# A two-block transformer kernel: attention rounds joined into one row of steps, and score matmuls on 64 partition rows

## The chip, the cores and the metric

One core of one Trainium2 chip runs the whole program. TensorE is called PE, VectorE DVE, ScalarE ACT, GpSimd POOL, SyncE SP. The metric is device time in microseconds (us) of one execution, median of several runs.

## The reference

Two transformer blocks on 512 tokens of 1024 channels, everything in float32. Of the first block only the three attentions matter here, of the second the sparse attention and a small cross attention:

```
A (diff_attention): 4 heads, each two maps of 64 channels; chunked causal mask
    p = softmax(q k^T * scale);  a = p[map 0] - lam * p[map 1];  o = a @ v (128 channels), then rmsnorm
B (chunk_band_attention): 8 heads of 64; a bias table for each head is added to the scores
C (memory_attention): 4 heads of 128, 256 memory rows
N (nsa_mixer): 16 heads of 64 in 4 groups that share keys and values; for each head
    o = g_c * softmax_c(q kc) vc + g_s * softmax_s(q ks) vs + g_w * softmax_w(q kw) vw
    c: 31 compressed keys; s: selected blocks (all, at this length); w: window (causal)
X (cross_attention): 4 heads of 64, 256 memory rows
```

Around them stand the projections, a gated recurrent branch and the feed-forward layers, which make up most of the time.

## The kernel before

The program is written engine by engine, in one order fixed by hand for each engine; semaphores join them. Projections are float32 split into a high and a low part, with three matmuls for one (`mm3`, L914 to L916): ACT rounds the raw weight tile (`act_split`, L621), DVE makes the rest (`dve_split`, L628), SP loads the next.

The attentions run in the order A, B, C, later N0, N1, X. Each is a loop over rounds (`its`: A 2, B 4, C 2, N0 2, N1 2, X 2), and a round has 16, 8, 8, 36, 36 and 8 steps. A step is one tile of 128 queries against all its keys for one head (and map or branch); `step_of` says which, `width` how many keys. A step goes through five stations:

1. PE: the score matmul into PSUM bank 4 + t % 4 (L733; L730 for the four small ones of a c step), once the bank's last step was read (`s_masked`).
2. DVE: adds the mask or bias, takes the row maximum and writes the scores to `Sm` (L865; c steps L854 to L857).
3. ACT: exp with the row sum (L790; c steps L784).
4. DVE: reciprocal (L890) and multiplication with it (L900 for B, C and X, L897 with a gate for N, L894 for A's second map, which also adds the first).
5. PE transposes it `lag` slots after the scores (L748; c steps L745; lag 4 for A, N, X, 3 for B, C), ACT copies the result to SBUF (`PT`, `PTr` or `PTnr`: L813, L810, L806).

When both steps of a map (in A and C all of a head's) are through, PE multiplies with the values two slots later (L1076 in A, L1084 for pairs of 64-wide heads in B, N and X, which write to two halves of the partitions, L1093 in C, L1104 in c steps); two slots after that ACT copies the output of a finished group (L836; in A L832, behind the squares of L829).

The slots run from 0 to the round's steps plus lag, so every round ends with its last transposes and products before the next begins. Ahead of a round DVE stages: `stage_a` to `stage_x` copy the queries (L1928, L1954, L1964, L2176, L2187) into four tiles `QZ` or `QZn`, of which the other 64 partition rows were set to zero by POOL (L503, L562), so that a matmul over 128 rows sees only one head's 64 channels; B and C also copy values into `vst` (L1955, L1965). PE waits for `staged` before its first slot. The bias tiles of B are made by POOL (L515) in two buffers, from two raw tiles that it loads itself. B's four rounds are a hardware loop; the other rounds are written out.

Of the kernel before, what the change touches and what calls it, by code (L numbers as in the profile page):

```python
# [107 lines left out]
def build(nc, a, out):  # L108

    ctx = ExitStack()  # L110
    with ctx:
# [59 lines left out]
        vst = place("vst", [P, TT, P], at=S_at + 10240)  # L171
# [31 lines left out]
        QZ = [place(f"QZ{s}", [P, T]) for s in range(4)]  # L203
        bias2 = [bias, place("bias1", [P, T])]
# [45 lines left out]
        top[0] = arena + 16384  # L250
        QZ2 = [place(f"QZn{s}", [P, T]) for s in range(4)]
# [172 lines left out]

        for n, its, steps, turns, maps, groups in (("A", 2, 16, 8, 2, 2), ("B", 4, 8, 8, 4, 1), ("C", 2, 8, 8, 2, 2),
                                                   ("N0", 2, 36, 36, 18, 2), ("N1", 2, 36, 36, 18, 2),
                                                   ("X", 2, 8, 8, 4, 1)):
            staged0 = attn_at[last]["stage0"] + attn_at[last]["its"] if attn_at else 0
            attn_at[n] = dict(its=its, n=steps, S0=atc[0], T0=atc[1], M0=atc[2], O0=atc[3], turns=turns, maps=maps, groups=groups, stage0=staged0)
            last = n  # L430
            atc = [atc[0] + its * steps, atc[1] + its * turns, atc[2] + its * maps, atc[3] + its * groups]
        s_full, s_taken, s_masked, s_exp, s_norm = (sem(x) for x in ("s_full", "s_taken", "s_masked", "s_exp", "s_norm"))
        t_full, t_free, pv_done, o_free, staged = (sem(x) for x in ("t_full", "t_free", "pv_done", "o_free", "staged"))
        bias_ready, pair_ready = sem("bias_ready"), sem("pair_ready")
        oa_sq, oa_sd, oa_ready = (sem(x) for x in ("oa_sq", "oa_sd", "oa_ready"))
        for n, per in (("A", 24), ("B", 8), ("C", 8), ("N0", 76), ("N1", 76), ("X", 8)):
            attn_at[n]["order"] = per
# [51 lines left out]
        def _(pool):  # L489
# [9 lines left out]
            for z in range(4):  # L499
                half = slice(64, 128) if z % 2 == 0 else slice(0, 64)  # L500

                pool.wait_ge(sq_used, 2 + 16) if z == 0 else pool.wait_ge(qz_zero, z)
                pool.memset(QZ[z][half, :], 0.0).then_inc(qz_zero, 1)  # L503

            for h in range(8 + 2):
                if h >= 2:
                    b = bias2[h % 2]
                    if h < 4:

                        pool.wait_ge(o_free, O_RING + attn_at["B"]["O0"])  # L510
                    else:

                        pool.wait_ge(s_masked, attn_at["B"]["S0"] + 8 * ((h - 2) // 2))
# [45 lines left out]
            for z in range(4):  # L559
                half = slice(64, 128) if z < 2 else slice(0, 64)  # L560
                pool.wait_ge(qz_zero, 4 + z)
                pool.memset(QZ2[z][half, :], 0.0).then_inc(qz_zero, 1)  # L562
            for h in range(2):
                pool.wait_ge(qz_zero, 8 + h)
                pool.memset(PTc[h][:, :], 0.0).then_inc(qz_zero, 1)
# [83 lines left out]
        def lag_of(kind):  # L649

            return 4 if kind in "ANX" else 3

        def S_of(kind, t):

            return Sm[t % (lag_of(kind) + 1)]

# [21 lines left out]
        def pt_of(kind, m):  # L678

            if not paired(kind):  # L680
                return PT[m % 2]
            if kind == "N" and m % 9 == 0:
                return PTc
            ring = PTr if kind == "B" else PTr2
            return [ring[:, m % 4, h, :] for h in range(2)]

        def group_of(kind, m):

            return m if kind in ("A", "C") else m // 9 if kind == "N" else 0

        def pt_free(A, kind, i, m):

            if not paired(kind):
                return M_(A, i, m) + (PV_RING - 1)
            if m < 4:

                return M_(A, i, 0) + PV_RING
            return M_(A, i, m) + (PV_RING - 3)

        def S_(A, i, t):  # L700
            return i * A["n"] + (A["S0"] + t)

        def T_(A, i, u):
            return i * A["turns"] + (A["T0"] + u)

        def M_(A, i, m):
            return i * A["maps"] + (A["M0"] + m)

        def O_(A, i, g):
            return i * A["groups"] + (A["O0"] + g)  # L710

        def pe_attention(pe, name, q_of, k_of, v_of):
            kind = name[0]
            A = attn_at[name]
            lag = lag_of(kind)
            stage0 = A["stage0"]

            def body(i):

                pe.wait_ge(staged, i + (stage0 + 1))  # L720
                for slot in range(A["n"] + lag):
                    if slot < A["n"]:
                        t = slot
                        h, m, qt = step_of(kind, t)
                        bank = ps[4 + t % 4]

                        pe.wait_ge(s_masked, S_(A, i, t) + (1 - S_RING)) if not (isinstance(i, int) and S_(A, i, t) < S_RING) else None
                        if m == "c":
                            for q in range(TT):
                                mm = pe.matmul(bank[:, q * NC32:(q + 1) * NC32], q_of(i, h, m, q), k_of(i, h, m, NC32), start=True, stop=True)  # L730
                        else:
                            n = width(kind, m, qt)
                            mm = pe.matmul(bank[:, 0:n], q_of(i, h, m, qt), k_of(i, h, m, n), start=True, stop=True)  # L733
                        mm.then_inc(s_full, 1)
                    t = slot - lag
                    if t >= 0 and turned(kind, t):
                        h, m, qt = step_of(kind, t)
                        u = turn_no(kind, t)
                        bank = ps[u % 2]

                        pe.wait_ge(s_norm, S_(A, i, t) + 1)
                        pe.wait_ge(t_free, T_(A, i, u) + 1)
                        if m == "c":
                            for q in range(TT):
                                mm = pe.transpose(bank[0:NC32, q * P:(q + 1) * P], S_of(kind, t)[:, q * NC32:(q + 1) * NC32], ident)  # L745
                        else:
                            for kc in range(width(kind, m, qt) // P):
                                mm = pe.transpose(bank[:, kc * P:(kc + 1) * P], S_of(kind, t)[:, kc * P:(kc + 1) * P], ident)  # L748
                        mm.then_inc(t_full, 1)

                    for te in ((t - 2, t - 1, t) if t == A["n"] - 1 else (t - 2,)):
                        m = last_of_map(kind, te) if te >= 0 else None
                        if m is None:
                            continue
                        g = group_of(kind, m)
                        u = turn_no(kind, te)

                        pe.wait_ge(t_free, T_(A, i, u) + (T_RING + 1))
                        if A["groups"] == 1:
                            if m == 0:  # L760
                                pe.wait_ge(o_free, O_(A, i, g) + O_RING)
                        elif kind != "N" or m % 9 == 0:
                            pe.wait_ge(o_free, O_(A, i, g) + 1)
                        obank = ps[2 + g % 2]
                        src = pt_of(kind, m)
                        mm = v_of(i, m, src, obank)
                        mm.then_inc(pv_done, 1)
            loop(pe, A["its"], body)

        def act_attention(act, name, o_to):  # L770
            kind = name[0]
            A = attn_at[name]
            lag = lag_of(kind)

            def body(i):
                for slot in range(A["n"] + lag - 1):
                    if slot < A["n"]:
                        t = slot
                        h, m, qt = step_of(kind, t)
                        n = width(kind, m, qt)  # L780

                        act.wait_ge(s_masked, S_(A, i, t) + 1)
                        if m == "c":
                            act.activation(S_of(kind, t)[:, 0:n], S_of(kind, t)[:, 0:n], ACT.Exp).then_inc(s_exp, 1)  # L784
                        else:
                            if m == "w":

                                at = (52 if qt == TT - 1 else 8) + t % 4
                                act.activation(st[:, 48 + t % 4:49 + t % 4], st[:, at:at + 1], ACT.Exp)
                            act.activation(S_of(kind, t)[:, 0:n], S_of(kind, t)[:, 0:n], ACT.Exp, bias=st[:, 8 + t % 4:9 + t % 4],  # L790
                                           scale=-1.0, accum_out=st[:, 12 + t % 4:13 + t % 4]).then_inc(s_exp, 1)
# [1512 lines left out]
```

## Time and profile before

| | us |
|---|---|
| median of 3 runs (2486.73 to 2488.80) | 2488.52 |
| the profiled execution | 2489.62 |
| its span, first to last instruction | 2487.8 |
| PE busy | 2324.6 (93%) |
| DVE busy | 1236.3 (50%) |
| ACT busy | 981.3 (39%) |
| POOL busy | 148.0 (6%) |
| matmuls of L914 to L916 in the chain that ended last | 70% |

The granted TensorE clock is 0.975 of full in the mean; a stretch shows it in tenths or as a share, where 0.5 is the lower of its two levels, 1.2 GHz of 2.4. Busy time counts a matmul from its start until its end has been modelled, so overlapping matmuls join into one piece; start times tell more than durations. Idle time is printed behind a row with what ended it.

### The profile page before, as it was taken

What the parts mean: (1) busy time and instruction counts of PE and PEld (TensorE: products, weight loads), DVE (VectorE), ACT (ScalarE), POOL (GpSimd) and SP (SyncE); (2) the same over time, 40 slices, a digit from 0 to 9 for tenths busy, and PEclk for the clock granted to TensorE, in tenths of its full rate; (3) what the DMA queues carried; (4) which work ended last, traced back from release to release, by engine and by line L of the source; (5) the groups of instructions that cost most, each with busy time, mean ns of one, the idle gap of its engine ahead of it and who ended that gap; (6) DMA issues with size and microseconds to landing.
All of it is one profiled execution on the core that took longest, in us unless ns stands there. A gap on an engine that the chain in (4) does not pass through costs nothing.

```text
span 2487.8 us, 30044 instructions
## 1 busy us (share of the span) xinstructions
PE 2324.6 (93%) x10984; PEld 1852.2 (74%) x10984; DVE 1236.3 (50%) x2264; ACT 981.3 (39%) x1621; POOL 148.0 (6%) x126
## 2 busy tenths in 40 slices
PE   5899999978887999999999989988999999999997
PEld 4788888766655777888888777766666688888886
DVE  4433335664455455444434647653888655432432
ACT  5432223454555333433223422623677633421321
POOL 1000002100010000100001420000000001000011
PEclk9999999989998999999999999999999999999998
DMA  5332333311200322332332372222000133233231
GB/s 186 105 101 76 110 95 88 112 52 43 68 9 26 101 93 93 102 101 79 107 100 79 90 233 80 68 71 76 14 1 1 42 95 101 86 102 101 85 101 51
DMA packets 213465, 206.72 MB, mean 83 GB/s; under 512 B 4832, under 2 KB 194400, under 8 KB 213120
## 3 DMA queue, kind: packets, MB, share of 16 engines
q1 hardware_dynamic: 210368, 192.31, 24.7%
q0 software_dynamic: 3008, 13.24, 1.6%
q8 instruction: 54, 0.88, 0.1%
q14 instruction: 35, 0.29, 0.0%
HBM read 199.25 MB, written 4.19 MB: 82 GB/s over the span
## 4 chain that ended last, share of the span: by engine, by line
PE 84%; DVE 8%; ACT 4%; issue 2%; DMA 2%; POOL 0%; SPq 0%; DVEq 0%; ACTq 0%; POOLq 0%
PE ps L914 24%; PE ps L916 23%; PE ps L915 23%; PE ps L733 4%; PE ps L1084 2%; PE ps L748 2%; DVE wlo L628 2%; ACT whi L621 2%; DMA wraw<-in_w_in 1%; DVE Sm L865 1%; PE ps L1119 1%; PE ps L730 1%; PE ps L1076 1%; DMA xin<-in_x 1%; PE ps L1144 0%
## 5 line engine op out<-in xcount | busy, mean ns | idle before, releaser
L628 DVE TENSOR_TENSOR wlo<-wraw,whi 128x2048 fp32r<-128x2048 f32 x192 | 440.4, 2294 | 425.1 <-ACT whi L621 425.1
L914 PE MATMUL ps<-hH,whi 128*128 128x512 f32 x1528 | 600.9, 393 | 19.0 <-DVE wlo L628 14.9
L916 PE MATMUL ps<-hH,wlo 128*128 128x512 f32 x1528 | 596.6, 390 | 0.0
L915 PE MATMUL ps<-hL,whi 128*128 128x512 f32 x1528 | 596.6, 390 | 0.0
L621 ACT ACTIVATE whi<-wraw 128x2048 fp32r<-128x2048 f32 x192 | 366.9, 1911 | 471.9 <-PE ps L916 441.3
L914 PEld LDWEIGHTS ps<-hH,whi 128*128 128x128 f32 x1528 | 287.6, 188 | 89.1 <-DVE wlo L628 21.6
L915 PEld LDWEIGHTS ps<-hL,whi 128*128 128x128 f32 x1528 | 287.7, 188 | 60.8 <-issue 1.0
L916 PEld LDWEIGHTS ps<-hH,wlo 128*128 128x128 f32 x1528 | 287.5, 188 | 61.0
L914 PE MATMUL ps<-gH,whi 128*128 128x512 f32 x608 | 236.5, 389 | 0.0
L915 PE MATMUL ps<-gL,whi 128*128 128x512 f32 x608 | 236.5, 389 | 0.0
L916 PE MATMUL ps<-gH,wlo 128*128 128x512 f32 x608 | 236.5, 389 | 0.0
L914 PE MATMUL ps<-whi,hH 128*128 128x512 f32 x352 | 140.9, 400 | 19.8 <-DVE wlo L628 9.4
L790 ACT ACTIVATE Sm<-Sm,st 128x128 f32<-128x128 f32 (+2 forms) x224 | 123.1, 550 | 45.9 <-DVE st L865 44.0
L915 PE MATMUL ps<-wlo,hH 128*128 128x512 f32 x352 | 139.4, 396 | 0.0
L916 PE MATMUL ps<-whi,hL 128*128 128x512 f32 x352 | 139.1, 395 | 0.0
L916 PEld LDWEIGHTS ps<-gH,wlo 128*128 128x128 f32 x608 | 114.1, 188 | 23.7
L915 PEld LDWEIGHTS ps<-gL,whi 128*128 128x128 f32 x608 | 114.1, 188 | 23.7
L914 PEld LDWEIGHTS ps<-gH,whi 128*128 128x128 f32 x608 | 114.1, 188 | 23.6
L748 PEld LDWEIGHTS ps<-cst,Sm 128*128 128x128 f32 x504 | 62.6, 146 | 88.7 <-issue 33.8
L748 PE MATMUL ps<-cst,Sm 128*128 128x128 f32 x504 | 94.3, 287 | 33.6 <-DVE Sm L894 14.4
L865 DVE CUSTOM_DVE_ANT_0 Sm<-ps,cst 128x128 f32<-128x128 f32 (+2 forms) x192 | 91.1, 475 | 32.8 <-PE ps L733 30.5
L1350 ACT ACTIVATE gH<-prod 128x512 f32 x44 | 27.8, 633 | 179.3 <-DVE prod L1754 179.3
(344 smaller groups left out, 2784.5 us busy)
## 6 DMA issues: line engine op xcount, KB each, us to landing
wraw<-in_w_in SPq DMA_DIRECT2D x45, 1024.0 KB, 5.0
wraw<-in_ffn_wg SPq DMA_DIRECT2D x22, 1024.0 KB, 5.1
wraw<-in_ffn_wu SPq DMA_DIRECT2D x22, 1024.0 KB, 5.1
wraw<-in_w_up SPq DMA_DIRECT2D x16, 1024.0 KB, 5.5
wraw<-in_w_down SPq DMA_DIRECT2D x16, 1024.0 KB, 5.2
wraw<-in_ffn_wd SPq DMA_DIRECT2D x16, 768.0 KB, 4.6
wraw<-in_w_gate SPq DMA_DIRECT2D x12, 1024.0 KB, 5.0
wraw<-in_ffn_wd SPq DMA_DIRECT2D x16, 640.0 KB, 4.2
```

What stands on the lines that cost most here:

```text
L621: act.activation(whi[s][:, :], wraw[s][:, :], ACT.Copy).then_inc(w_hi[s], 1)
L628: dve.tensor_tensor(wlo[s][:, :], wraw[s][:, :], f32(whi[s][:, :]), ALU.subtract).then_inc(w_lo[s], 1)
L730: mm = pe.matmul(bank[:, q * NC32:(q + 1) * NC32], q_of(i, h, m, q), k_of(i, h, m, NC32), start=True, stop=True)
L733: mm = pe.matmul(bank[:, 0:n], q_of(i, h, m, qt), k_of(i, h, m, n), start=True, stop=True)
L748: mm = pe.transpose(bank[:, kc * P:(kc + 1) * P], S_of(kind, t)[:, kc * P:(kc + 1) * P], ident)
L790: act.activation(S_of(kind, t)[:, 0:n], S_of(kind, t)[:, 0:n], ACT.Exp, bias=st[:, 8 + t % 4:9 + t % 4], scale=-1.0, accum_out=st[:, 12 + ...
L865: scored = dve.tensor_tensor_reduce(s_[:, 0:n], ps[4 + t % 4][:, 0:n], mask_of(t, n), -1.0, 0.0 if m == "w" and qt < TT - 1 else 3e38, ALU ...
L914: pe.matmul(o, lh, rh, start=start, stop=False)
L915: pe.matmul(o, lh, rl, start=False, stop=False)
L916: return pe.matmul(o, ll, rh, start=False, stop=stop)
L1084: mm = nc.tensor.matmul(ob[HD * h:HD * h + HD, qt * P:(qt + 1) * P], val(h, kc), src[h][:, kc * P:(kc + 1) * P], start=start and kc == 0, ...
L1350: act.activation(gH[:, i * 2 + g, :], prod[g][:, :], ACT.Copy).then_inc(g_hi, 1)
```

## The change

All rounds of A, of B and of C become one row of steps each, and those of N0, N1 and X one row together. A class `Step` holds what a step needs: its index k in the row (for the `Sm` ring, k % (lag + 1)), its counts over the whole program (s for score banks, u for transposes, M for maps, G for output groups), and the rings are counted through by these. Each engine's function walks the row once: a step of the next round follows the last one of this round in the next slot, and transposes, products and output copies of the old round run between the new one's. Everything is written out, B too.

The tiles `QZ`, `QZn` and `vst`, their copies, the POOL memsets of them and the semaphore `staged` are gone. PE reads both operands of a score matmul from 64 partition rows of the projections' own tiles (`rows_of`), rows 0 to 63 or 64 to 127; C, with 128 channels, takes all rows of `QT` and `mkT`. B's and C's values are read from `Vt` and `mv`. PE waits for the key tile's copies out of PSUM (`turns_over`). B's bias has four buffers, each free when the score steps of the head two rounds earlier are done.

```diff
-        QZ = [place(f"QZ{s}", [P, T]) for s in range(4)]
-        bias2 = [bias, place("bias1", [P, T])]
+        bias4 = [bias] + [place(f"bias{s}", [P, T]) for s in range(1, 4)]
...
-        def pe_attention(pe, name, q_of, k_of, v_of):
-            def body(i):
-                pe.wait_ge(staged, i + (stage0 + 1))
-                for slot in range(A["n"] + lag):
...
+        class Step:
+            def __init__(self, name, i, t, k):
...
+                self.s = i * A["n"] + A["S0"] + t
+                self.bank, self.c = ps[4 + self.s % 4], self.s % 4
+                self.Sm = Sm[k % (lag_of(kind) + 1)]
...
+        def pe_attention(pe, names, q_of, k_of, v_of):
+            seq, lag = steps(names)
+            last = len(seq) - 1
+            for slot in range(len(seq) + lag):
+                if slot <= last:
+                    e = seq[slot]
+                    if e.s >= S_RING:
+                        pe.wait_ge(s_masked, e.s + 1 - S_RING)
...
+                        mm = pe.matmul(e.bank[:, 0:e.n], q_of(e, e.qt), k_of(e, e.n), start=True, stop=True)
+                    mm.then_inc(s_full, 1)
...
-            pe_attention(pe, "A", lambda i, h, m, q: QZ[2 * h + m][:, q * P:(q + 1) * P],
-                         lambda i, h, m, n: KT[:, i * 2 + h, 0:n], pv_a)
+            turns_over("ak")
+            pe_attention(pe, ["A"], lambda e, q: QT[rows_of(e.m), e.i * 2 + e.h, toks(q)],
+                         lambda e, n: KT[rows_of(e.m), e.i * 2 + e.h, 0:n], pv_a)
...
-            pe_attention(pe, "B", lambda i, h, m, q: QZ[h][:, q * P:(q + 1) * P],
-                         lambda i, h, m, n: KT[:, i, 0:n], pv_b)
+            turns_over("bk")
+            pe_attention(pe, ["B"], lambda e, q: QT[rows_of(e.h), e.i, toks(q)], lambda e, n: KT[rows_of(e.h), e.i, 0:n], pv_b)
...
-            def stage_b(i):
-                dve.wait_ge(pv_done, M_(attn_at["B"], i, 0) + PV_RING)
-                for h in range(2):
-                    r = slice(HD * h, HD * h + HD)
-                    dve.tensor_copy(QZ[h][r, :], QT[r, i, :])
-                dve.tensor_copy(vst[:, :, :], Vt[:, :, bass.ds(i * P, P)]).then_inc(staged, 1)
...
+                return q2[rows_of(e.h // 2), 4 * int(e.name[1]) + 2 * e.i + e.h % 2, toks(q)]
...
+                return kcT[rows_of(e.h // 2), aa, :] if e.m == "c" else kT2[rows_of(e.h // 2), (2 if e.m == "w" else 0) + aa, 0:n]
+            pe_attention(pe, ["N0", "N1", "X"], q_of, k_of, pv_nx)
```

## Rows read from the trace of the kernel before

**Rows 1.** The table of stretches: A, B, B's last round, C, N with X.

```profile
core 0: us, PE busy (x) PEld busy (x) DVE busy (x) ACT busy (x) POOL busy (x), PEclk, DMA share, GB/s
525.20:587.70 62.50, 43.15 (x184) 30.89 (x185) 38.27 (x153) 33.07 (x118) 0.01 (x1) 0.81 0.05 17
666.70:730.60 63.90, 46.19 (x304) 30.07 (x305) 41.62 (x140) 39.03 (x104) 9.95 (x10) 0.92 0.08 25
717.90:730.60 12.70, 10.53 (x76) 6.55 (x77) 7.52 (x32) 8.99 (x26) 0.00 (x0) 1.00 0.00 0
763.40:792.00 28.60, 22.60 (x81) 13.48 (x81) 15.55 (x72) 17.60 (x55) 0.00 (x0) 0.87 0.03 9
1738.90:1970.70 231.80, 218.37 (x1568) 143.79 (x1568) 188.58 (x805) 162.11 (x539) 0.58 (x1) 0.98 0.04 15
```

**Rows 2.** Timeline where N begins: DVE, then PE (start, us, instruction, idle before).

```profile
1738.92 1.52 DVE L2176 COPY QZn<-q 64x512 f32<-64x512 f32 x4
1742.45 0.29 DVE L854 TENSOR_TENSOR Sm<-ps,cst 128x128 f32<-128x128 f32 x1 [2.01 <-PE ps L730]
...
1740.50 3.62 PE L730 MATMUL ps<-kcT,QZn 128*128 128x32 f32 x16 [7.75 <-DVE QZn L2176]
...
1746.08 1.04 PE L745 MATMUL ps<-cst,Sm 128*32 128x128 f32 x4
```

**Rows 3.** Timeline of DVE at the end of a round of B.

```profile
693.75 2.05 DVE L900 TENSOR_SCALAR Sm<-Sm,st 128x512 f32<-128x512 f32 x1
```

**Rows 4.** Timeline of PE in N, around the boundary near 1840 and before.

```profile
1787.69 1.02 PE L733 MATMUL ps<-kT,QZn 128*128 128x512 f32 x2
...
1814.99 1.02 PE L733 MATMUL ps<-kT,QZn 128*128 128x512 f32 x2
...
1839.38 1.02 PE L733 MATMUL ps<-kT,QZn 128*128 128x512 f32 x2
...
1840.92 0.55 PE L748 MATMUL ps<-cst,Sm 128*128 128x128 f32 x3
...
1846.83 1.97 PE L730 MATMUL ps<-kcT,QZn 128*128 128x32 f32 x16
...
1850.77 0.61 PE L745 MATMUL ps<-cst,Sm 128*32 128x128 f32 x4 [1.00 <-DVE Sm L885]
```

**Rows 5.** Timeline of DVE in A.

```profile
528.00 0.29 DVE L865 CUSTOM_DVE_ANT_0 Sm<-ps,cst 128x128 f32<-128x128 f32 x1 [1.04 <-PE ps L733]
...
537.30 0.29 DVE L865 CUSTOM_DVE_ANT_0 Sm<-ps,cst 128x128 f32<-128x128 f32 x1 [0.22 <-DVE Sm L900]
...
549.74 0.16 DVE L890 RECIPROCAL st<-st 128x1 f32<-128x1 f32 x1 [1.31 <-ACT Sm L790]
...
556.74 0.29 DVE L865 CUSTOM_DVE_ANT_0 Sm<-ps,cst 128x128 f32<-128x128 f32 x1 [4.22 <-PE ps L733]
```

**Rows 6.** Timeline of PE in C, start of the second round.

```profile
779.18 1.99 PE L733 MATMUL ps<-mkT,QZ 128*128 128x256 f32 x8 [1.26 <-DVE vst L1965]
```

**Rows 7.** Timeline of PE in N, away from a boundary.

```profile
1860.03 0.70 PE L733 MATMUL ps<-kT,QZn 128*128 128x256 f32 x2
1860.57 0.60 PE L748 MATMUL ps<-cst,Sm 128*128 128x128 f32 x4
1861.01 0.60 PE L733 MATMUL ps<-kT,QZn 128*128 128x256 f32 x2
1861.44 0.60 PE L748 MATMUL ps<-cst,Sm 128*128 128x128 f32 x4
1861.97 0.88 PE L1084 MATMUL ps<-PTnr,v 128*64 128x128 f32 x12
```

**Rows 8.** Timeline of PE at the only matmuls on fewer rows.

```profile
1730.47 1.91 PE L1037 MATMUL ps<-cst,tk 128*128 128x128 f32 x16
1732.31 0.44 PE L1259 MATMUL ps<-cst,ngT 48*128 48x48 f32 x4
...
1500.88 0.30 PE L1131 MATMUL ps<-cst,kct 31*128 31x31 f32 x2
1501.11 0.50 PE L914 MATMUL ps<-hH,whi 128*128 128x512 f32 x1
```

More of the change, by code:

```diff
@@ L248, in build @@
         yacc = xc
-        top[0] = arena + 16384
-        QZ2 = [place(f"QZn{s}", [P, T]) for s in range(4)]
+        top[0] = arena + 24576
         PT2_at = top[0]
@@ L558, in _ @@
             pool.wait_ge(y1_done, DC)
[L559 to L562, printed above, removed]
             for h in range(2):
-                pool.wait_ge(qz_zero, 8 + h)
+                if h:
+                    pool.wait_ge(qz_zero, h)
                 pool.memset(PTc[h][:, :], 0.0).then_inc(qz_zero, 1)
@@ L676, in last_of_map @@
             return t // 2 if t % 2 == 1 else None
[L678 to L710, printed above, removed]
-        def pe_attention(pe, name, q_of, k_of, v_of):
[L713 to L716, printed above, removed]
-            def body(i):
-                pe.wait_ge(staged, i + (stage0 + 1))
-                for slot in range(A["n"] + lag):
[L722 to L730, printed above, removed]
-                        else:
[L732 to L768, printed above, removed]
@@ new lines, in build, with pt, pt_free @@
+        class Step:
+            def __init__(self, name, i, t, k):
+                A = attn_at[name]
+                self.name, self.kind, self.i, self.k = name, name[0], i, k
+                kind = self.kind
+                self.h, self.m, self.qt = step_of(kind, t)
+                self.first = t == 0
+                self.s = i * A["n"] + A["S0"] + t
+                self.bank, self.c = ps[4 + self.s % 4], self.s % 4
+                self.Sm = Sm[k % (lag_of(kind) + 1)]
+                self.n = width(kind, self.m, self.qt)
+                self.turned = turned(kind, t)
+                self.u = i * A["turns"] + A["T0"] + turn_no(kind, t)
+                self.tbank = ps[self.u % 2]
+                ends = [x for x in range(t, A["n"]) if last_of_map(kind, x) is not None]
+                self.map = last_of_map(kind, ends[0])
+                self.ends_map = ends[0] == t
+                self.M = i * A["maps"] + A["M0"] + self.map
+                group = self.map if kind in ("A", "C") else self.map // 9 if kind == "N" else 0
+                self.g = group
+                self.G = i * A["groups"] + A["O0"] + group
+                self.obank = ps[2 + self.G % 2]
+                self.starts_group = kind in ("A", "C") or self.map % 9 == 0
+                self.ends_group = kind in ("A", "C") or self.map == (8 if kind == "N" else 3) or self.map == 17
+            def pt(self):
+                if not paired(self.kind):
+                    return PT[self.M % 2]
+                if self.m == "c":
+                    return PTc
+                ring = PTr if self.kind == "B" else PTr2
+                return [ring[:, self.M % 4, h, :] for h in range(2)]
+            def pt_free(self):
+                return self.M + PV_RING - (3 if paired(self.kind) else 1)
@@ new lines, in steps @@
+        def steps(names):
+            at = [(n, i, t) for n in names for i in range(attn_at[n]["its"]) for t in range(attn_at[n]["n"])]
+            return [Step(n, i, t, k) for k, (n, i, t) in enumerate(at)], lag_of(names[0])
+        def pe_attention(pe, names, q_of, k_of, v_of):
[6 more added lines that the diff above has]
+                        pe.wait_ge(s_masked, e.s + 1 - S_RING)
+                    if e.m == "c":
+                        for q in range(TT):
+                            mm = pe.matmul(e.bank[:, q * NC32:(q + 1) * NC32], q_of(e, q), k_of(e, NC32), start=True, stop=True)
+                    else:
+                        mm = pe.matmul(e.bank[:, 0:e.n], q_of(e, e.qt), k_of(e, e.n), start=True, stop=True)
+                    mm.then_inc(s_full, 1)
+                t = slot - lag
+                if t >= 0 and seq[t].turned:
+                    e = seq[t]
+                    pe.wait_ge(s_norm, e.s + 1)
+                    pe.wait_ge(t_free, e.u + 1)
+                    if e.m == "c":
+                        for q in range(TT):
+                            mm = pe.transpose(e.tbank[0:NC32, q * P:(q + 1) * P], e.Sm[:, q * NC32:(q + 1) * NC32], ident)
+                    else:
+                        for kc in range(e.n // P):
+                            mm = pe.transpose(e.tbank[:, kc * P:(kc + 1) * P], e.Sm[:, kc * P:(kc + 1) * P], ident)
+                    mm.then_inc(t_full, 1)
+                for te in ((t - 2, t - 1, t) if t == last else (t - 2,)):
+                    if te < 0 or not seq[te].ends_map:
+                        continue
+                    e = seq[te]
+                    pe.wait_ge(t_free, e.u + T_RING + 1)
+                    if e.starts_group:
+                        pe.wait_ge(o_free, e.G + 1)
+                    v_of(e, e.pt(), e.obank).then_inc(pv_done, 1)
@@ L1634, in _ @@
             act_split(act, S, 1, 0)
[L1635 to L1637 removed]
+            act.wait_ge(qz_zero, 2)
+            act_attention(act, ["N0", "N1", "X"],
+                          lambda e: ox[:, e.i, :] if e.kind == "X" else yn[:, 4 * int(e.name[1]) + 2 * e.g + e.i, :])
             act.wait_ge(o_free, O_RING + attn_at["X"]["O0"] + 2)
```

349 lines of the change are left out of this document (146 added, 203 removed).

## The prediction

> **What bounds the kernel now.** The page's chain comes first: most of it is TensorE in the projections' three-product matmuls, which the change does not touch. So I asked the table of stretches for those it does touch: attention A (525.2 to 587.7), B (666.7 to 730.6), C (763.4 to 792.0), and N0, N1 and X in one (1738.9 to 1970.7), 386.8 us in all [rows 1]. In the last one PE is busy 218 of 232 us, DVE 189, ACT 162: PE sets the pace. In A, B and C it is busy 43 of 62.5, 46 of 63.9 and 22.6 of 28.6: they lose time to something else. Then the timeline, for what a step costs and what lies between rounds. S is a score matmul, T a group of transposes, PV probabilities times values; xn counts PE's records, and T has one for each 128 columns.
>
> **Part 1: the copies go (L1928, L1954, L2176, L2187).** Four take DVE 1.52 us before a round of N [rows 2]. They matter where everybody waits for them, at a round's start, so they are priced with the boundaries. The POOL memsets lie under other work: nothing. The bias tiles on POOL get four buffers instead of two; the additions of heads 4 to 7 still fall into B, and while POOL adds, a DVE multiplication of some 0.5 us takes 2.05 [rows 3]. I leave 1 us for them.
>
> **Part 2: rounds become one row of steps.** What a boundary costs:
>
> - N: the last S of 512 columns starts at 1787.69, the one in the middle of the next round at 1814.99, that round's last at 1839.38 [rows 4]. So 18 steps without a boundary take 24.4 us, 18 with one 27.3: a boundary is 2.9. What makes it up stands behind 1839.38: T and PV that are left, the c scores from 1846.83, and a wait of 1.00 for DVE ahead of T. N's rounds and X make four such boundaries, 11.6; between X's two rounds, which are shorter, I take 1.3. Saved: 12.9.
> - N's start: DVE ends its copies at 1740.4 but scores first at 1742.45, since PE's S starts behind them, at 1740.50, and slowly [rows 2]. Afterwards PE does S while DVE still splits weights, and DVE can score at 1739.0: 3.5 earlier. The first T comes 5.6 behind the first S (1746.08), in a later round 3.9 (1846.83 to 1850.77, rows 4): another 1.7. Saved: 5.2.
> - A is paced by DVE. Head 0 takes it from 528.00 to 537.30, 9.3; head 1 until 549.74, 12.4, since PV on PE and the squares on ACT get in its way; the next round scores first at 556.74 [rows 5]. In one row heads 1, 2 and 3 all look like head 1: 9.3 + 3 x 12.4 = 46.5, against 556.74 + 9.3 + 12.4 - 528.00 = 50.4 now. That is 3.9 less, not the 7.0 of the gap, because PV and squares that lie in the gap come back in the stream. The copies ahead of the first S give 2 (four of 0.4, and the way to them). Saved: 6.
> - B: its last round starts at 717.9 and hands over at 730.6, with PE busy 10.5 of 12.7 [rows 1]; I take 10.2 as PE's work in a round. The three before it take 51.2, 17.1 each. In one row: four times 10.2 and part 3's 2.0, 48.8; 1.3 to fill and empty; 0.8 to hand over; 0.5 for slow first matmuls; 1 for POOL: 52.4. From about 666.0, when K is turned, that ends at 718.4 instead of 730.6. Saved: 12.2. DVE is busy 7.5 in a round, so PE becomes the bound.
> - C: the second round's first S starts at 779.18 [rows 6], so the rounds take 15.8 (with 1.2 of copies) and 12.8, for PE's 22.6 / 2 = 11.3, part of that at the lower clock. One drain and one start of the two go, about 3.8 by what the second round has over its PE work and the wait of 1.26; the copies give 1.2. Saved: 5.
>
> Parts 1 and 2: 12.9 + 5.2 + 6 + 12.2 + 5 = 41.3 saved.
>
> **Part 3: S takes 64 rows, T keeps 128.** S has as many columns as before; halving its rows makes nothing shorter. But now S and T differ in shape on the array, and PE alternates between them. The trace has such alternations, between T (128\*128) and PV (128\*64). S of 256 columns takes 0.54 to the next instruction behind PV (1860.03), 0.43 behind T (1861.01): 0.11 more. T x4 takes 0.44 ahead of S (1860.57) and 0.53 ahead of PV (1861.44): 0.09 more, in which nothing overlaps [rows 7]. And T x3 behind PV lasts 0.55 (1840.92, rows 4), where x4 lasts 0.60 and a record more is 0.11: 0.06 more. So a change of shape costs 0.09 ahead of it, and behind it 0.06 (T) or 0.11 (S): S to T 0.15, T to S 0.20. Do rows count as shape? Sixteen full transposes and then the 48-row ones take 1.84, 0.10 over 16 x 0.109; and behind 31 rows a full matmul lasts 0.50, where the page's mean for its line is 0.39 [rows 8]. Both show the same price, so I use it for 64 rows.
>
> How many? A map is S T S T PV. Now only PV is entered and left; then S to T, T to S, S to T are added: 2 x 0.15 + 0.20 = 0.50. N has 72 maps and X 8: 80 x 0.50 = 40.0 us, where PE has no room. Waits inside N's steps I put at 0.5 in 18 steps, so 4 are absorbed. B has 4 maps in a round: 2.0, used above. In A the two maps' S lie side by side, one pair of changes for two steps, 0.35, behind a DVE that needs 2.3 for them: nothing. C stays at 128 rows.
>
> The Trainium skill, "TensorEngine Tiling (Array Packing)", Tiling Modes, says that changing the tiling mode drains TensorE. It speaks against this change, the 48-row and 31-row rows agree, and it gives no price; without it the sum would be the rival "free". The skill's "TensorE: Matmul & The Clock Gate", Part 3, says that matmuls on different row groups run at once; no row here shows it. By it A's S pairs would halve, some 2 us at most where DVE waits for them.
>
> **Sum.** 2488.5 - 41.3 + 40.0 - 4.0 = 2483.2, say **2483**: A -6, B -12, C -5, N and X +18. The profiled execution took 2489.6 (span 2487.8), 1.1 over the median of 2488.5; all terms are differences, so I take them from the median. Bounds: A 3 to 9 saved; B 10 to 15; C 4 to 6.5; N and X +12 (more waits absorbed, changes at 0.14) to +21 (none absorbed). All good: 2470; all bad: 2492.5.
>
> **Rivals.** A measurement of this kernel tells from no change about 0.2%, 5 us.
>
> - *Free*: 64 rows drain nothing. N and X keep their gain of 18.1, B gains 8 more: 2488.5 - 41.3 - 8 + 1 (POOL and DVE take over in B) = 2440. For it: each row witness is a single place. Against: both show the full price. Chance 0.08.
> - *Dearer*, the slower side: on 64 rows the second record of an S waits until the first has left the array, a third 0.10 for each of 176 S of N, X and B: +17.6, 2501. It decides from 0.06 on (11 us, slower by 5). The skill's clock gate page, Part 3, says that a weight load overlaps a running matmul only if the row group differs, which would do this. Against: four 48-row transposes take 0.44 with their loads [rows 8], and on 128 rows the two records of an S follow each other without a gap. Chance 0.12.
> - *Boundaries give little*: DVE, ACT or a ring takes the drain's place. A, B and C keep half of their 23: 2494. For it: A's head 1. Against: in B's 63.9 us PE, DVE and ACT are busy 46, 42 and 39 [rows 1]. Chance 0.10.
> - The forecast: 0.70; its own range is 2473 to 2492, about evenly on either side of 2483.5, where faster begins.
>
> Range 2468 to 2495: it leaves out "free" (0.08) and most of "dearer" (0.10). Faster: 0.36 + 0.08 + 0.01 = 0.45. Same: 0.31 + 0.01 + 0.02 = 0.34. Slower: 0.03 + 0.11 + 0.07 = 0.21.
>
> **What to look for.** In N, S of 256 columns takes 0.63 to the next T (0.54, and 0.09 ahead of T), T x4 lasts 0.65 rather than 0.60, 18 steps take 28.4 instead of 24.4, and no gap is left where rounds met. B lasts about 52 us with PE busy nearly throughout, A 57, C 24, N with X some 18 more than now. I am wrong if T and S alternate at 0.11 as before (free), if that S takes 0.73 (dearer), or if B stays over 57.

## The result, and the profile after

The changed kernel takes 2537.03 us in the median of four runs (2527.52 to 2545.77), against 2487.89 for the kernel before beside it: ratio 1.0196, 95% interval 1.0167 to 1.0225. It is slower by 2%, 54 us above the forecast of 2483 and outside its range. The profiled execution is the longest, 2545.77 us (span 2543.7, mean clock 0.947); that of before took 2489.62 (clock 0.975). The four runs order by their clock: 2545.77 at 0.947, 2537.25 and 2536.81 at 0.951, 2527.52 at 0.955.

I cut both traces at the last projection matmul ahead of an attention and the first behind it:

| us | before | after | difference | forecast |
|---|---|---|---|---|
| A | 67.64 | 64.49 | -3.2 | -6 |
| B | 69.90 | 89.17 | +19.3 | -12 |
| C | 39.72 | 34.17 | -5.6 | -5 |
| N with X | 240.50 | 287.26 | +46.8 | +18 |
| all the rest | 2070.1 | 2068.6 | -1.5 | 0 |

So all of the loss lies in B and in N with X. The table of stretches of the changed kernel, for A, B, C, N with X, and then three pieces of the last one:

```profile
core 0: us, PE busy (x) PEld busy (x) DVE busy (x) ACT busy (x) POOL busy (x), PEclk, DMA share, GB/s
521.70:586.20 64.50, 45.40 (x203) 30.15 (x201) 37.19 (x145) 37.30 (x124) 0.02 (x1) 0.71 0.09 32
659.10:748.20 89.10, 83.84 (x322) 43.29 (x320) 36.86 (x129) 40.03 (x107) 6.33 (x6) 0.56 0.04 12
769.90:804.00 34.10, 25.06 (x98) 16.25 (x96) 19.22 (x74) 25.28 (x66) 0.00 (x0) 0.85 0.05 16
1739.30:2026.60 287.30, 278.82 (x1591) 156.03 (x1589) 190.34 (x787) 176.91 (x547) 0.57 (x1) 0.87 0.05 16
...
1757.00:1805.00 48.00, 48.00 (x171) 25.24 (x171) 21.41 (x87) 17.82 (x59) 0.00 (x0) 0.50 0.00 1
1807.00:1884.00 77.00, 77.00 (x480) 42.54 (x479) 59.09 (x244) 53.93 (x171) 0.00 (x0) 1.00 0.00 1
...
1884.90:1895.10 10.20, 10.20 (x53) 6.71 (x52) 4.87 (x23) 3.94 (x12) 0.00 (x0) 0.50 0.01 2
```

Compare the column PEclk with [rows 1]: B had 0.92 and has 0.56, N with X had 0.98 and has 0.87. In the 48 us from 1757 PE never idles, hardly anything is transferred (1 GB/s), and the granted clock is 0.50, TensorE's lower level of 1.2 GHz; in the 77 us from 1807 PE never idles either and the clock is 1.00, 2.4 GHz. Added up from the trace's clock records, the clock was at its lower level for 78.5 us in B (10.2 before) and 75.1 in N with X (13.7 before), 61.4 of them in one piece from 1745.0.

Where the clock is up, the steps look as they were forecast. The timeline of PE in N of the changed kernel, away from the start:

```profile
1990.66 0.66 PE L729 MATMUL ps<-cst,Sm 128*128 128x128 f32 x4
1991.25 0.70 PE L716 MATMUL ps<-kT,q 64*128 64x256 f32 x2
1991.87 0.66 PE L729 MATMUL ps<-cst,Sm 128*128 128x128 f32 x4
```

S of 256 columns takes 0.62 to the next T, and T x4 lasts 0.66, where 0.63 and 0.65 were named. In A the S of the two maps, on the two row halves, run at once, for which the prediction had no row: four records of 512 columns take 1.06 to the next T.

```profile
544.69 1.13 PE L716 MATMUL ps<-KT,QT 64*128 64x512 f32 x4
545.75 0.44 PE L729 MATMUL ps<-cst,Sm 128*128 128x128 f32 x2
```

And this is how N starts, in the same view; the number in brackets is PE's idle time before the row:

```profile
1742.28 1.97 PE L714 MATMUL ps<-kcT,q 64*128 64x32 f32 x16 [0.47 <-ACT kT L1389]
1744.08 0.69 PE L716 MATMUL ps<-kT,q 64*128 64x128 f32 x4
1751.70 1.03 PE L726 MATMUL ps<-cst,Sm 128*32 128x128 f32 x4 [6.92 <-DVE Sm L830]
1752.66 1.22 PE L716 MATMUL ps<-kT,q 64*128 64x256 f32 x2
1753.81 1.03 PE L726 MATMUL ps<-cst,Sm 128*32 128x128 f32 x4
```

PE idles 6.92 us until the first probabilities come, comes back at the lower clock (the same S takes 1.15 instead of 0.62), and stays there for 54.7 us of unbroken work, until 1806.4.

### The profile page after: what moved, and what is told of

It is laid out like the page before. It is cut to its first block, busy times and chain, and to the rows that moved or that the text cites. A ratio compares the mean times of both kernels' runs of the same rounds, so it can differ in the third digit from the quotient of the medians.

```text
span 2543.7 us, 29730 instructions
## 1 busy us (share of the span) xinstructions
PE 2416.4 (95%) x10984; PEld 1871.1 (74%) x10984; DVE 1222.7 (48%) x2216; ACT 984.0 (39%) x1618; POOL 144.6 (6%) x118
## 4 chain that ended last, share of the span: by engine, by line
PE 87%; DVE 5%; ACT 4%; DMA 2%; issue 1%; POOL 0%; SPq 0%; ACTq 0%; DVEq 0%; POOLq 0%
PE ps L858 23%; PE ps L860 23%; PE ps L859 23%; PE ps L716 7%; PE ps L729 4%; PE ps L1033 3%; DVE wlo L613 2%; ACT whi L606 2%; DMA wraw<-in_w_in 1%; PE ps L714 1%; PE ps L1025 1%; PE ps L1073 1%; DMA xin<-in_x 1%; PE ps L726 0%; PE ps L1098 0%
## 5 line engine op out<-in xcount | busy, mean ns | idle before, releaser
L729 PE MATMUL ps<-cst,Sm 128*128 128x128 f32 x504 | 117.9, 339 | 16.0 <-DVE Sm L839 13.9
L716 PE MATMUL ps<-kT,q 64*128 64x128 f32 (+3 forms) x256 | 114.8, 533 | 0.0
```

What stands on the lines that cost most here:

```text
L716: mm = pe.matmul(e.bank[:, 0:e.n], q_of(e, e.qt), k_of(e, e.n), start=True, stop=True)
L729: mm = pe.transpose(e.tbank[:, kc * P:(kc + 1) * P], e.Sm[:, kc * P:(kc + 1) * P], ident)
```

## The experiments

Theory 1: 64-row score matmuls are what keeps TensorE at the lower clock; the price of the shape changes was right. Rivals: the merged row of steps does it by its order or its waits; the shape changes themselves do it; the halved rows cost something else. Lengths of stages below are cut as in the table above, from each profiled execution.

**All rows, merged steps** (e1_full_rows).

```diff
-  QT[rows_of(e.m), e.i * 2 + e.h, toks(q)], KT[rows_of(e.m), e.i * 2 + e.h, 0:n]
+  QT[:, e.i * 2 + e.h, toks(q)],            KT[:, e.i * 2 + e.h, 0:n]
   (and so in B, N and X)
```

> The changed kernel with the score matmuls of A, B, N and X back on all 128 partition rows of both operands, so that one row of steps without rounds and copies is all that is left of the change (computation changed: a score then sums the products of two heads' rows). First theory (the merging of the rounds gives what was forecast, and the 64-row score matmuls cost both the shape changes and the granted clock): B about 53 us, N+X about 222 us, in all 2447 us, and the granted clock in B and in the first 60 us of N at 0.9 or more. Rival (the merged row of steps itself, through its waits or its order, is what lowers the clock): B stays at about 89 us at a clock of 0.5, the time stays above 2510 us.

Measured: 2446.68 us (2446.13 to 2448.46), ratio 0.9831 [0.9815, 0.9848], clock 0.979. A 60.1, B 52.4, C 32.9, N with X 231.4. Its start of N, the same view:

```profile
1703.69 0.69 PE L716 MATMUL ps<-kT,q 128*128 128x128 f32 x4
1711.30 1.04 PE L726 MATMUL ps<-cst,Sm 128*32 128x128 f32 x4 [6.92 <-DVE Sm L830]
1712.13 1.06 PE L716 MATMUL ps<-kT,q 128*128 128x256 f32 x2
1712.98 1.06 PE L726 MATMUL ps<-cst,Sm 128*32 128x128 f32 x4
...
1715.72 0.27 PE L729 MATMUL ps<-cst,Sm 128*128 128x128 f32 x1
```

The same idle time of 6.92, the same slow first matmuls, but a transposition takes 0.27 again from 1715.72 on, and the table of stretches has 1.00 for all that follows:

```profile
1698.90:1715.60 16.70, 9.30 (x57) 7.49 (x56) 8.74 (x30) 10.12 (x20) 0.00 (x0) 0.69 0.41 126
1715.60:1930.30 214.70, 207.88 (x1534) 136.97 (x1533) 176.34 (x757) 160.60 (x528) 0.57 (x1) 1.00 0.03 11
```

Merging is cleared: without the 64 rows, merging (with the copies gone) saves 41 us, and the stretch at 1.2 GHz at N's start is 10.2 us long. The total met the expectation and N with X did not: 231.4 where 222 was named.

**64 rows, rounds kept** (e2_before_64_rows).

```diff
-  lambda i, h, m, q: QZ2[h][:, q * P:(q + 1) * P], k_of         (k_of: kT2[:, ...])
+  lambda i, h, m, q: QZ2[h][rows_of(h // 2), q * P:(q + 1) * P], k_of   (kT2[rows_of(h // 2), ...])
   (and so in A and X; in B QZ[0][rows_of(0), ...] and KT[rows_of(0), 0, 0:n])
```

> The kernel before, rounds and copies kept, with the score matmuls of A, B, N and X on 64 partition rows of both operands (in B both heads read the first head's query tile and key tile 0: computation changed there). First theory (the clock goes with the 64 rows): the shape changes add 40 to 44 us and the clock falls to 0.5 in parts of B and N for another 20 to 60, in all 2550 to 2590 us. Rival (the shape changes are all that 64 rows cost, the merged row of steps lowers the clock): 2528 to 2532 us at the clock of before.

Measured: 2642.6 us (2629.12 to 2652.07), ratio 1.0626 [1.0576, 1.0675], even above what theory 1 said; N with X alone takes 360.9, of which 228.7 at the lower clock. Its table of stretches, for 55 to 58 us behind the start of N and behind the three other starts of a round:

```profile
1758.00:1816.00 58.00, 50.35 (x167) 27.36 (x167) 29.17 (x111) 23.11 (x66) 0.00 (x0) 0.53 0.08 25
1845.00:1900.00 55.00, 53.16 (x220) 28.97 (x218) 29.49 (x121) 22.61 (x71) 0.00 (x0) 0.58 0.00 1
1928.00:1983.00 55.00, 53.28 (x216) 29.44 (x218) 28.67 (x118) 22.69 (x73) 0.00 (x0) 0.57 0.00 1
2009.00:2065.00 56.00, 54.17 (x227) 29.91 (x227) 29.60 (x122) 23.39 (x73) 0.00 (x0) 0.57 0.00 1
```

Each of the three boundaries inside N, with waits of 0.84 and 1.0 us on PE, starts another stretch of 55 us at 1.2 GHz. So 64 rows do it without the merging, and the merging spares the changed kernel three of these four falls. Against the 64 rows of this kernel merging is worth 106 us.

**Shape changes on full rows** (e3_column_halves).

```diff
-  mm = pe.matmul(e.bank[:, 0:e.n], q_of(e, e.qt), k_of(e, e.n), start=True, stop=True)
+  for w in range(2):      # 64 queries, all rows; C as before
+      c_ = slice(64 * w, 64 * w + 64)
+      mm = pe.matmul(e.bank[c_, 0:e.n], q_of(e, e.qt)[:, c_], k_of(e, e.n), start=True, stop=True)
```

> The first of these kernels, but each score matmul of A, B, N and X is cut into two of 64 queries, each on all 128 rows and on half of the output's partitions (computation changed in the same way), so that the shape changes of the changed kernel are there and the halved rows are not. If the halved rows lower the clock and shape changes do not: 2447 us plus some 40 for the shape changes and up to 28 for the second matmul (208 matmuls of 0.13 us on average), 2487 to 2515 us, with a clock of 0.9 or more in B. If it is the shape changes that lower the clock: above 2530 us with B at 0.5.

Measured: 2463.06 us (2459.67 to 2464.66), ratio 0.99 [0.9884, 0.9917], clock 0.98; B 55.9, N with X 241.8, of these 6.8 and 10.2 at the lower clock. The timeline of PE in N:

```profile
1854.80 0.66 PE L731 MATMUL ps<-cst,Sm 128*128 128x128 f32 x4
1855.38 0.65 PE L718 MATMUL ps<-kT,q 128*64 128x256 f32 x4
1855.97 0.66 PE L731 MATMUL ps<-cst,Sm 128*128 128x128 f32 x4
1856.55 0.88 PE L1035 MATMUL ps<-PTnr,v 128*64 128x128 f32 x12
1857.26 0.60 PE L718 MATMUL ps<-kT,q 128*64 128x256 f32 x4
```

The shape changes between S and T are there (T x4 lasts 0.66 as in the changed kernel) and the clock stays up: the shape changes do not lower it. The time came out below the range given: the two halves run at once (four records of S in 0.59 to the next T, where two on full rows take 0.43 [rows 7]; the other 0.16 is the shape changes, for which the prediction has 0.20), so the second matmul costs nothing, and between PV and S, now of one shape, nothing is paid. These shape changes cost 16 us in all over the kernel on full rows.

**Padded keys** (e4_padded_keys): full rows, with zeroes in the other head's half of the keys.

```diff
-  act_turned(act, "ak", 4, lambda c: KT[:, c, :])
+  for c in range(n):
+      act.wait_ge(turn_full, c0 + c + 1)
+      for h in range(2):              # rows of head h into a tile whose other rows are zero
+          r = rows_of(h)
+          mm = act.activation(KZ[4 * h + c][r, 0:w], ps[4 + (c0 + c) % 4][r, 0:w], ACT.Copy, scale=scale)
+      mm.then_inc(turn_free, 1)
+  (so in A, B and N; POOL zeroes the other halves; queries are read as QT[:, ...], q2[:, ...])
```

> The changed kernel with full-row score matmuls that compute the right thing without staging copies: ScalarE writes each turned key tile as two half-height copies into two tiles whose other halves GpSimd has zeroed, and the query tiles are read as they are; only X keeps 64 rows. First theory (all that the change loses comes from 64-row matmuls): the 2447 us of the merged kernel on full rows, plus some 5 us for X's shape changes and 2 to 4 us for 12 more copies ahead of A, B and N, 2450 to 2460 us, faster than both kernels. Rival (the merged steps lower the clock): above 2510 us.

Measured: 2463.7 us (2461.39 to 2464.62), ratio 0.9902 [0.9885, 0.9918]: faster than both kernels, 3.7 above the range given. It is 17 above the first experiment in the median and 13 in the span: A 5.0 more, B 3.1, N with X 6.0, C and the rest 1 less. The clock is at its lower level for 6.8 us in B and 13.7 in N with X, about as before the change, though half of the key rows hold zeroes: it was enough here that the matmul ran over all rows, whatever stood in them.

**Pairs back to back** (e5_pairs_back_to_back).

```diff
-  if slot <= last:
-      e = seq[slot]
+  if slot <= last and slot % 2 == 0:
+      es = seq[slot:slot + 2]                       # heads or maps on rows 0-63 and 64-127
+      pe.wait_ge(s_masked, es[-1].s + 1 - S_RING)
+      for e in es: mm = pe.matmul(...); mm.then_inc(s_full, 1)
 (DVE's step waits for t_full of the Sm tile's last reader)
```

> The changed kernel, with the two 64-row score matmuls of a pair of steps issued back to back, one on rows 0 to 63 and one on rows 64 to 127, and then two steps of transposes (computation changed in N: the second head of a pair takes the other group's rows, so that the pair lies on both row halves there too). If what lowers the clock is that a 64-row matmul leaves half of the array's rows idle, and two of them on different halves run together as the column halves of probs times values do: the clock is at 0.95 or more in B, score time halves (some 28 us of 56 less than on full rows), half the shape changes of the experiment with column halves stay (8 us), in all 2425 to 2435 us. If they do not run together: B at 0.5 and the time above 2500 us.

Measured: 2437.95 us (2435.89 to 2438.47), ratio 0.9796 [0.978, 0.9813], 3 above the range; A 64.5, B 50.3, N with X 217.9. The timeline of PE in N, then the stretches of B and of N with X:

```profile
1785.31 0.61 PE L730 MATMUL ps<-cst,Sm 128*32 128x128 f32 x4 [0.32 <-DVE Sm L836]
1785.85 0.70 PE L719 MATMUL ps<-kT,q 64*128 64x256 f32 x4
1786.48 0.61 PE L730 MATMUL ps<-cst,Sm 128*32 128x128 f32 x4
```

```profile
659.40:709.70 50.30, 41.84 (x323) 24.48 (x321) 35.81 (x129) 39.52 (x107) 6.33 (x6) 0.93 0.07 22
1701.90:1919.80 217.90, 194.29 (x1590) 113.87 (x1589) 184.55 (x787) 170.75 (x547) 0.57 (x1) 0.97 0.06 21
```

Two S of 256 columns (four records) now take 0.63 together, what one takes in the changed kernel, and the clock is up in B and N. The shape is the same 64\*128; what differs is that both halves of the rows are at work.

**Fillers in the idle stretches** (e6_padded_filled on the padded kernel, e7_after_filled on the changed one).

```diff
+  def fill(n, name=None):
+      if name: nc.tensor.wait_ge(mm_free[0], free_after(stages[name], 0, 0))
+      for _ in range(n):
+          nc.tensor.matmul(ps[0][:, :], ident, C("mask_chunk"), start=True, stop=True)
...
+  fill(13, "bv")
   turns_over("bk")
   pe_attention(pe, ["B"], ...          # 12, 13 and 7 for A, C and N
...
+  if slot == lag: fill({"A": 4, "B": 3, "C": 2, "N": 9}[names[0][0]])
```

> The correct kernel with padded keys, and TensorE's idle stretches at the start of A, B, C and N filled with 45 plus 18 plain 128x512 matmuls on full rows whose results nobody reads. If the clock falls at these starts because TensorE idles: of the 27, 7, 7 and 14 us at 1.2 GHz most go, which gives back up to half of them, 2440 to 2455 us. If not, or if the fillers hold up the first steps: 2460 to 2475 us.

> The changed kernel, 64-row score matmuls as they are, with the same fillers. Theory that the start decides (a stretch that begins at 1.2 GHz stays there, one that begins at 2.4 GHz stays there too): B at 57 us, N+X at 245 us, in all 2470 to 2490 us. Theory that the mix of matmuls decides (64-row score matmuls keep activity too low whatever came ahead): B again at 80 us or more with a clock near 0.5, in all 2510 to 2540 us.

Measured: the padded kernel 2476.96 us (2474.74 to 2477.75), ratio 0.9954 [0.9937, 0.9971], 13 worse than without fillers and 2 above the range even for fillers that hold up the first steps, although B, C and N have no microsecond at the lower clock any more. I had taken a filler for 0.43 us; each is two records of 0.43, so they held up the first steps (B 61.0 instead of 55.5). The changed kernel 2514.81 us (2508.81 to 2535.96), ratio 1.0136 [1.0088, 1.0185]: above the range of the theory that the start decides, for the same reason, and inside that of its rival. But the rival's long stretch near 0.5 is not there: the profiled execution, of 2508.81, shows just what the theory of the start says of the clock (B 65.7 and N with X 263.2, both at 1.00; the three longer runs have clocks of 0.981 to 0.97):

```profile
663.00:728.70 65.70, 63.06 (x355) 33.46 (x353) 36.52 (x129) 41.17 (x107) 6.34 (x6) 1.00 0.06 17
1726.80:1990.00 263.20, 262.12 (x1623) 146.65 (x1621) 189.65 (x787) 177.87 (x547) 0.57 (x1) 1.00 0.05 17
```

**Pairs in A, B and X, padded keys in N** (e8_pairs_in_ab_padded_n): the edit of the pairs in the first three, that of the padded keys in N.

> A correct kernel: in A, B and X the two 64-row score matmuls of a pair back to back on both row halves, in N the padded keys. If pairs run together at the full clock: A and B some 6 and 7 us under the padded kernel's 65 and 55, no padding copies ahead of them, in all 2445 to 2455 us. If they do not: B above 80 us and 2490 us or more.

Measured: 2452.53 us (2451.25 to 2454.12), ratio 0.9859 [0.9843, 0.9876]. B is 50.3, 5.1 under the padded kernel; A is 64.3, only 0.9 under it, not 6: in A the changed kernel (64.5) has its pairs together already, as the two lines from 544.69 showed, so the edit changes little there. Pairs alone do not keep A's clock up either: it is at the lower level for 37.5 of its 64 us, as in the changed kernel, against 17.7 on full rows.

**Fillers cut in half** (e9_after_half_filled, e10_pairs_half_filled): the counts are 6, 7, 7 and 4 ahead of A, B, C and N, and 1, 1, 0 and 5 at slot lag.

> The changed kernel with the fillers cut to what the idle stretches hold: each plain 128x512 matmul takes 0.86 us and not 0.43, so 6, 7, 7 and 4 ahead of the first steps of A, B, C and N and 1, 1, 0 and 5 ahead of the first transposes. Theory that the start decides for 64-row score matmuls: no long stretch at 1.2 GHz in B or N, B 57 to 60 us, N+X 257 to 262 us, in all 2478 to 2488 us, which is what was forecast for the change. Theory that the long fillers themselves held the clock in the kernel with twice as many: a long cold stretch in B or N comes back, above 2505 us.

> The correct kernel with pairs in A, B and X and padded keys in N, with the same halved fillers. If the fillers now only cover idle time: the 7, 7 and 14 us at 1.2 GHz in B, C and N give back up to half, 2438 to 2450 us. If they still delay the first steps: 2452 us or more.

Measured, the changed kernel: 2490.04 us (2483.06 to 2496.03), ratio 1.0012 [1.0002, 1.0021]; the profiled execution is the one of 2483.06, at a clock of 0.982. In its timeline the fillers (L708) have taken the place of the idle time, and S takes 0.63 from the first on:

```profile
1714.63 0.69 PE L723 MATMUL ps<-kT,q 64*128 64x128 f32 x4
1715.25 4.56 PE L708 MATMUL ps<-cst 128*128 128x512 f32 x10
1719.64 0.60 PE L735 MATMUL ps<-cst,Sm 128*32 128x128 f32 x4
1720.17 0.70 PE L723 MATMUL ps<-kT,q 64*128 64x256 f32 x2
1720.80 0.61 PE L735 MATMUL ps<-cst,Sm 128*32 128x128 f32 x4
```

```profile
520.30:585.10 64.80, 47.65 (x216) 29.97 (x214) 37.21 (x145) 37.30 (x124) 0.00 (x0) 0.79 0.10 33
656.50:715.80 59.30, 56.47 (x339) 30.43 (x337) 36.44 (x129) 41.02 (x107) 6.35 (x6) 1.00 0.07 19
737.40:769.20 31.80, 27.71 (x112) 15.57 (x111) 19.14 (x74) 24.64 (x66) 0.00 (x0) 1.00 0.06 18
1706.80:1963.90 257.10, 256.04 (x1608) 143.87 (x1607) 189.70 (x787) 178.09 (x547) 0.58 (x1) 1.00 0.05 18
```

Profile against profile that is 62.7 us less than the changed kernel (2545.77), and the stages say where: B 29.9, N with X 30.1, C 2.4, A -0.4, the rest 0.6. More matmuls and less time. These two profiles are the slowest of four executions and the fastest of eleven; the medians lie 47 us apart. The other runs are up to 13 us longer than the profiled one at clocks down to 0.976, so the clock fell in some of them too; the median is 2 above the range given. On the pairs kernel the fillers bring nothing that counts: 2451.2 us (2448.98 to 2453.24), 1 above the range given, ratio 0.9852 [0.9839, 0.9866] where it had 0.9859.

**Full rows at the start only** (e11_first_round_full), no fillers; **pairs on one half in N** (e12_pairs_n_one_half).

```diff
-  q2[rows_of(e.h // 2), ...]
+  q2[slice(0, P) if (e.name, e.i) == ("N0", 0) else rows_of(e.h // 2), ...]      # e11; in B e.i == 0
-  q2[rows_of(e.h % 2), ...]
+  q2[rows_of(e.h // 2), ...]                                                      # e12, against the pairs back to back
```

> The changed kernel without fillers, with the score matmuls of the first eight steps of B and of the first 36 steps of N on all 128 rows and all later ones on 64 (computation changed in those steps: both heads' rows are summed). If a stretch with 64-row score matmuls only fails to leave the low clock, but keeps the high one: the full-row steps bring the clock back after some 7 to 14 us as in the kernel on full rows, B 57 to 62 us, N+X 255 to 263 us, in all 2485 to 2500 us. If it is the fillers' cover of the idle time and nothing else that kept the clock: long stretches at 0.5 in B or N, above 2510 us.

> The back-to-back kernel with N computed rightly: in A, B and X the pairs still lie on both row halves, in N both of a pair lie on the same half and can't run together. If idle rows are what keeps the clock low: B at 50 us at the high clock, but in N a stretch of 30 us or more at 1.2 GHz, N+X 265 us or more, in all 2485 us or more. If it is only the number of shape changes or the order: N+X near 240 us with 14 us at the low clock, in all some 2460 us.

Measured, full rows at the start: 2505.26 us (2504.69 to 2506.26), ratio 1.0077 [1.006, 1.0093], between the two theories, because the two stages part:

```profile
659.10:676.50 17.40, 12.27 (x72) 7.76 (x70) 12.75 (x40) 14.27 (x34) 3.65 (x4) 1.00 0.14 46
676.50:738.50 62.00, 62.00 (x226) 31.90 (x224) 23.76 (x91) 24.54 (x73) 2.68 (x2) 0.50 0.02 5
659.10:741.10 82.00, 76.12 (x323) 41.18 (x321) 36.52 (x129) 40.09 (x107) 6.33 (x6) 0.63 0.05 13
1732.20:1985.80 253.60, 244.39 (x1591) 143.47 (x1589) 188.86 (x787) 176.12 (x547) 0.58 (x1) 0.97 0.05 18
```

In N it went as the start theory says: full rows bring the clock up after 10.2 us at the lower level, the 108 steps of N that follow and X run on 64 rows with 3.4 us at it, and N with X takes 253.5 without a filler. In B the clock was up at first and fell at 676.7, behind two waits of PE of 0.36 and 0.88 us at the start of the second round; then it stayed down for 61.4 us, until 738.1 near the end of B, with PE busy all the time. That goes against the other half of the start theory: a stretch that begins at the high clock does not always keep it.

Measured, pairs on one half in N: 2489.99 us (2476.58 to 2499.89), ratio 1.0006 [0.9989, 1.0023]. B is 50.3 with 6.8 us at the lower clock, N with X 271.9 with 78.5. One kernel holds both cases, and the one stage where pairs share a half of the rows is the one that stays down, for 54.6 us in its first piece:

```profile
1707.00:1762.00 55.00, 48.22 (x170) 27.30 (x171) 29.27 (x111) 21.55 (x68) 0.00 (x0) 0.50 0.06 20
```

## Why the prediction was wrong

The step that failed is the one that is not in the sum: all terms of part 3 were taken at the clock of [rows 7], and N's and B's stretches at the clock of [rows 1], as if what PE does could not change what it is granted. PE idles at each start in both kernels; in B and N the lower clock behind it lasts 3 to 14 us in the kernel before and 61 to 79 in the changed one, and with its score matmuls back on full rows 3 to 10. By the half-filled kernel that costs 60 us in B and in N with X, 62.7 in all, in the profiled execution, the slowest one (2545.8, 62.8 above the forecast of 2483); between the medians it is 47 of the 54 that the forecast missed. None of the rivals had it, and [rows 4] and [rows 7], read at the high clock, could not show it; the lower PEclk of A, B and C in [rows 1] was there to be asked about.

By the forecast's own terms:

- **Shape changes on 64 rows, +40, 4 of it absorbed.** The price of one is right: S 0.62, T x4 0.66. In the half-filled kernel 18 steps of N take 28.18 from c step to c step, where 28.4 was named. But the kernel on full rows takes 25.18 and not 24.4, so the difference is 3.0 and not 4.0. Part of that falls into waits of PE (6.8 of 214.7 us on full rows, 1.1 of 257.1 here); the rest is not accounted for. N with X pays 25.7 (257.2 against 231.4), not 36; B 6.9 rather than 8, A 4.7 where nothing was expected. Between these two kernels that is 37.3 for the three stages, fillers included and by the fastest execution of the filled one.
- **Boundaries and copies, -41.3.** B's 12.2 in it already had 8 of shape changes taken off, so for the kernel on full rows the terms amount to 49.3. It saves 41 in the median: N with X 9.1 and not 18.1, B 17.5 and not 20.2, A 7.5, C 6.9. That it met my expectation of 2447, which took 41.3 as it stands, is luck. In N the mistake was the one I had avoided in A: the interval of 27.3 less one of 24.4 was called the price of a boundary, though the T, PV and c scores in it come back in the stream. From c step to c step the kernel before takes 21.40 and 30.30 in turn, 25.85 in the mean, against 25.18 merged: 0.67 for 18 steps, 5.4 for eight times 18. N's start gave 3.4 of 5.2 (last projection matmul to first T, 15.84 to 12.41).
- So N with X at the high clock is 16.7 above before in the half-filled kernel, where 18 was forecast, by two errors of 9 and 10 that cancel. It is luck, too, that this kernel's fastest execution, 2483.06, meets the forecast of 2483: A and B save 3.2 and 1.4 less than forecast, C 2.9 more.
- **A.** -3.2 with 37.5 us of its 64.5 at the lower clock; on full rows 17.7 and -7.5. "Nothing" for its shape changes may even be right: with column halves A has them too and takes 59.0, with 10.2 us at the lower clock. That puts the 4.7 down to the clock rather (27.3 us at the lower level in the half-filled kernel), but no run separates the two.
- **B, 52.4 long.** On full rows 52.4, but that is without the shape changes and from the last projection matmul on, so the same number by accident; with them and at the high clock 59.3, where the forecast amounts to 57.7 in this measure (69.9 - 12.2). On 64 rows, left alone, 89.2.
- **C**: -5.6 against -5.
- **Free** and **dearer** are both out. S of 512 columns behind PV takes 1.06 to the next T on 64 rows (1852.09 to 1853.15 in the half-filled kernel) and 0.96 on full rows (0.53 and 0.43 for its two records): 0.10 more, the change ahead of T, and nothing between its records. The overlap rule that the rival "dearer" quoted from the Trainium skill, "TensorE: Matmul & The Clock Gate", Part 3, does not show as a cost here. **Boundaries give little** held in N alone, for another reason than a new wait.

The Trainium skill's same page, Part 1, says that a TensorE without work is throttled and that sustained activity releases it. The first half agrees with the starts here; by the second the 48 us from 1757, busy from end to end, should have been at 2.4 GHz, and the trace has 0.50. The measurement decides: in the long stretches of this kernel, 78.5 us in B and 61.4 in N, being busy did not bring the clock back sooner, and in both each S used one half of the rows alone.

What stays open: what makes the clock fall in the first place. In B with 64 rows it fell behind waits of 0.36 and 0.88 us in one kernel and did not fall behind 0.22 and 0.88 in the half-filled one; in the changed kernel it fell for 10.2 us at 1884.9 among c steps with no wait at all. Why a low stretch behind a start in N ends after 55 to 65 us, and that one after 10.2, was not tried either, nor whether S on one half of the rows is enough by itself or only among these transposes and products.

## What to carry to other kernels

Where a change puts fewer partition rows through TensorE, read the granted clock by stretches, after as well as before, and look at where TensorE idles ahead of the stretch: the price of the change can be the clock and not the instructions. If operands have 64 rows, issue the two halves back to back, so that they run at once (the pairs took the time of one, and kept the clock in B and N, though not in A, where PE waits for DVE in every head); if only one half can be had, pad it to 128 rows on the side that is copied anyway. Of the kernels that leave the computation as it is, the fastest does both, at 2452.5 us (2451.2 with the fillers), 1.4% under the kernel before and 3.3% under the changed one. And to price a boundary between rounds, compare whole periods (from c step to c step), not an interval with it to one without: work that lies in the gap comes back.

## What the hardware showed unexpectedly

- Two matmuls of shape 64\*128 on different row halves, and two of 128\*64 on different column halves, run at once: four records of 256 columns in 0.63 and 0.59 us, shape change included. The Trainium skill's "TensorEngine Tiling (Array Packing)", Tiling Modes, says that tiles work in parallel; the traces agree.
- The same instruction stream has two paces, by the clock. In N of the changed kernel 18 steps take 28.18 us from 1825.66 to 1853.84, and 47.96 from 1742.28 to 1790.24, of which PE idled 6.92.
- Adding 31 matmuls (62 records) that do nothing, in idle stretches, made the changed kernel 47 us faster in the median (2490.04 against 2537.03).
